# Border changes in a one-core diffusion layer kernel: the order of loads in the first stage, work moved across stage borders, and the end of the output projection

## Chip, cores and metric

The kernel runs on one core of a Trainium2 chip. The metric is the device time in microseconds (us) of one execution. PE is TensorE, DVE is VectorE, ACT is ScalarE, POOL is GpSimd, SP is SyncE, which issues most of the DMAs.

## The reference

One layer of a hybrid diffusion model, in float32: 1024 latent tokens `x` and 256 context tokens `ctx`, 1024 channels wide. Cut to what matters here:

```python
sh1, sc1, g1, sh2, sc2, g2 = modulation(c, w_mod)      # silu(c) @ w_mod + b_mod, in six parts
u_l = modulate(x, norm_g[0], sh1, sc1) @ w_in          # rmsnorm(x) * g * (1 + sc1) + sh1
u_c = modulate(ctx, norm_g[0], sh1c, sc1c) @ w_in      # the same for the context, with c_ctx
# four mixers over column groups of u: GLA, Hyena, Mamba-2, gated DeltaNet
# the end of DeltaNet: head_rmsnorm(o, dn_norm) * silu(og)
# Hyena: x2 * long_conv(x1 * long_conv(v, h0), h1), v, x1, x2 from a conv of three taps,
#        filters h from a three-layer sine network, times a decay window
y = concatenate([gla, hyena, mamba, deltanet]) @ w_out
x = x + g1 * rmsnorm(y, norm_g[1])
h = rmsnorm(x, norm_g[2]) * (1 + sc2) + sh2
x = x + g2 * rmsnorm(ec_moe(h), norm_g[3])             # 16 experts, each takes its best tokens
```

The mixture `ec_moe` takes the softmax over the 16 columns of `h @ moe_router` as affinities, and each expert picks the tokens with the largest.

## The kernel before, in words

The program (L3281) is a row of stages. Each `Stage` is a block of five instruction streams, one for each engine, which are synchronised by semaphores alone and joined by a barrier at its end. Within a stage each engine works through its list in the order written; there is no planner, so what stands before an instruction on its engine is what is written before it. The stages, in order: `mod` (function `modulate`, L197), GLA's two (`gla`, L764), Mamba's, DeltaNet's (`deltanet`, L1423, its scan is the stage `dn_s`, L1779), Hyena's (`hyena`, L2378: `hy_c`, `hy_f`, `hy_d`), `out` (`project_out`, L2734), `moe` (`experts`, L2970) and `fin` (`finish`, L3229).

**mod.** SP issues (L217 to L237), all in one order: for each of eight pieces of `w_mod` (1 MB each) first the token tiles that go with it (tiles 0 to 5 with pieces 0 to 5, tiles 6 and 7 with piece 6, 8 and 9 with piece 7; 0.5 MB each), then the piece; then the mixer weights of GLA (800 columns, 3.2 MB) and two narrow column blocks of 8 and 16 columns, 1024 rows each. The ring of token tiles has four buffers, so tile t waits at L224 until DVE has normalised tile t - 4. ACT squares each tile (L277), DVE scales it (L316), PE turns it with eight transposes (L362), ACT and DVE copy the two halves out (L285, L322). PE multiplies each piece with `silu(c)` (L375). Behind all of them come the row copies (L299 on ACT, L334 on DVE), the 16 transposes that make columns of the modulation rows (L388), and DVE's reduces and adds (L343 to L349).

**gla's first stage.** PE (L849) waits for all mixer weights at once; ACT (L896) and DVE (L944) first scale and shift `hT` by the modulation.

**dn_s.** Ten steps of 128 tokens, both directions in each, are PE products, with ACT and DVE copying between them (ACT: L2020, L2026, L2033; DVE: L2090 writes the output). POOL takes differences of `h` in the earlier steps. **hy_c** is a `project_conv` (L443): six blocks of 128 columns, each product in three passes over a high and a low part of `w` and `hT` (L547 to L549); ACT makes the high part of the first block in four quarters (L527), DVE the low part (L534). Beside it runs `HeadNorm` for DeltaNet's output: ACT's Silu of the gate (L692), POOL's product of gate and weights (L734), DVE's square (L719), reduce, division (L724) and gate product (L729), and 16 transposes (L742) on PE behind the products of block 0. `FilterLayers` (L2306) computes the sine network on the side. Each block's convolution is ACT's centre tap (L633) and two DVE operations (L668, L672), and ACT copies it to `yT` (L595).

**hy_f.** PE makes the filter taps (L2470, L2476), DVE windows them (L2506) and adds the skip at L2514, and PE, ACT and DVE do the transform (L2453, L2563).

**out.** For each of eight tiles of 128 tokens: PE 48 matmuls of 128x512 (L2830 to L2832), ACT the square and root (L2884, L2886), DVE the scaling (L2925), POOL the addition of x, which gives `x1` (L2795), ACT square and root of that (L2889, L2891), DVE the scaling to `h` (L2936), POOL the shift row (L2798). PE turns `h` (L2806) after the next product, multiplies it with the router (L2818) in the middle of the one after, and DVE and ACT take the softmax (L2910 to L2913) whose transpose (L2826) DVE stores (L2945). SP stores `h`. For the last tile DVE does POOL's two additions (L2930, L2940).

**moe and fin.** SP feeds the expert weights through a ring. `fin` loads the sums and the gate row (L3239), and takes the last norm and the residual, tile by tile (L3261 to L3278).

## Time and profile before

| | |
|---|---|
| median of 3 runs | 1836.09 us (1835.57 to 1836.58) |
| the profiled execution | 1830.56 us, its span 1828.7 us |
| mean granted clock of PE | 0.931 |
| DMA over the span | 340.19 MB, 186 GB/s |
| first work of gla's first stage | 54.01 us |
| of hy_f | 888.64 us |
| of moe | 1167.61 us |
| first row load of fin | 1797.63 us |

A time stands in us from the start of the span. "Busy" is the union of an engine's instructions. An idle time stands in front of the instruction that ended it, together with what released it.

### The profile page before, as it was taken

Reading aid. Unit: us, or ns where it says so; the run is one execution under the profiler, and the core shown is the slowest. Engines: PE = TensorE matmul, PEld = TensorE weight load, DVE = VectorE, ACT = ScalarE, POOL = GpSimd, SP = SyncE. Lnnn points to the kernel's source line nnn. Section 1 sums busy time; section 2 is a strip of 40 time slices with the busy share of each in tenths; the row PEclk is TensorE's granted clock in tenths of the full one; section 3 lists DMA queues with packets and bytes.
Section 4 is the critical chain, followed back from the end, with each engine's and each line's share of the span. In section 5 each row is a group of like instructions: output and inputs, shape, how many; then the busy total and the mean of one; then the engine's idle time right before and its main releaser. Section 6 shows DMA issues by size and latency. Waiting matters only on the chain. (4 is left out here: it accounts for less than half of the span.)

```text
span 1828.7 us, 20488 instructions
## 1 busy us (share of the span) xinstructions
PE 1581.6 (86%) x7747; PEld 1179.7 (65%) x7747; DVE 1169.1 (64%) x1338; ACT 887.4 (49%) x1219; POOL 345.1 (19%) x404
## 2 busy tenths in 40 slices
PE   5899999988998869989877799239999999999981
PEld 2454665466556658868457578238888888888860
DVE  3640562249354655765679623678888888888863
ACT  4230334334426546643110245327777777777752
POOL 0000320055002768710000144001001001001001
PEclk9889999988998979999999899569999999999986
DMA  9740200041003753330321422339999999999957
GB/s 365 241 164 1 93 1 0 0 145 41 0 1 106 235 162 91 102 104 0 115 92 39 159 104 81 161 138 375 395 399 384 393 399 394 385 400 395 380 194 206
DMA packets 103000, 340.19 MB, mean 186 GB/s; under 512 B 36295, under 2 KB 41034, under 8 KB 78327
## 3 DMA queue, kind: packets, MB, share of 16 engines
q1 hardware_dynamic: 93022, 315.09, 45.4%
q0 software_dynamic: 5328, 18.88, 4.2%
q10 hardware_dynamic: 4553, 4.92, 1.0%
q8 instruction: 62, 1.02, 0.2%
q14 instruction: 35, 0.29, 0.0%
HBM read 301.52 MB, written 37.32 MB: 185 GB/s over the span
## 5 line engine op out<-in xcount | busy, mean ns | idle before, releaser
L3165 DVE TENSOR_TENSOR w_lo<-w_raw,w_hi 128x2048 fp32r<-128x2048 f32 x192 | 438.4, 2292 | 65.4 <-ACT w_hi L3107 65.4
L3107 ACT ACTIVATE w_hi<-w_raw 128x2048 fp32r<-128x2048 f32 x192 | 368.1, 1918 | 144.6 <-PE ps L3057 134.1
L566 PE MATMUL ps<-hT,w_mixer 128*128 128x512 f32 (+1 forms) x576 | 225.2, 551 | 3.4 <-PEq L177 1.7
L3055 PE MATMUL ps<-w_hi,xsT_hi 128*128 128x512 f32 x512 | 202.8, 396 | 2.4 <-DVE xsT_lo L3170 2.4
L3057 PE MATMUL ps<-w_hi,xsT_lo 128*128 128x512 f32 x512 | 200.4, 391 | 0.0
L3056 PE MATMUL ps<-w_lo,xsT_hi 128*128 128x512 f32 x512 | 200.2, 391 | 0.0
L566 PEld LDWEIGHTS ps<-hT,w_mixer 128*128 128x128 f32 x576 | 109.5, 192 | 110.1 <-issue 106.8
L3023 POOL DMA_INDIRECT moe_sum<-y,idx_col x15 | 30.6, 2040 | 460.7 <-ACT y L3127 460.7
L3055 PEld LDWEIGHTS ps<-w_hi,xsT_hi 128*128 128x128 f32 x512 | 96.8, 189 | 22.0 <-DVE xsT_lo L3170 2.8
L3057 PEld LDWEIGHTS ps<-w_hi,xsT_lo 128*128 128x128 f32 x512 | 96.5, 189 | 20.4
L3056 PEld LDWEIGHTS ps<-w_lo,xsT_hi 128*128 128x128 f32 x512 | 96.7, 189 | 19.3
L3055 PE MATMUL ps<-w_hi,hiddenT_hi 128*128 128x512 f32 x256 | 100.5, 392 | 2.4 <-DVE hiddenT_lo L3182 2.4
L3056 PE MATMUL ps<-w_lo,hiddenT_hi 128*128 128x512 f32 x256 | 100.3, 392 | 0.0
L3057 PE MATMUL ps<-w_hi,hiddenT_lo 128*128 128x512 f32 x256 | 100.2, 392 | 0.0
L888 PE MATMUL ps<-w_mixer,hT 128*128 128x512 f32 (+1 forms) x160 | 64.1, 564 | 0.6 <-ACT mb_dt L925 0.6
L2789 POOL TENSOR_TENSOR yT_lo<-yT,yT_hi 128x1024 fp32r<-128x1024 f32 x7 | 18.5, 2637 | 227.7 <-ACT yT_hi L2869 227.7
L2830 PE MATMUL ps<-w_out_hi,yT_hi 128*128 128x512 f32 x128 | 52.7, 412 | 7.9 <-DVE w_out_lo L2904 5.2
L623 ACT ACTIVATE mb_c_line<-ps 128x512 f32<-128x512 f32 (+1 forms) x20 | 18.2, 909 | 84.5 <-PE ps L566 84.5
L3055 PEld LDWEIGHTS ps<-w_hi,hiddenT_hi 128*128 128x128 f32 x256 | 48.6, 190 | 12.9 <-DVE hiddenT_lo L3182 2.8
L3056 PEld LDWEIGHTS ps<-w_lo,hiddenT_hi 128*128 128x128 f32 x256 | 48.5, 189 | 10.1
L3057 PEld LDWEIGHTS ps<-w_hi,hiddenT_lo 128*128 128x128 f32 x256 | 48.5, 189 | 10.1
L849 PE MATMUL ps<-hT,w_mixer 128*128 128x512 f32 (+1 forms) x128 | 50.1, 554 | 4.7 <-DVE hT L944 4.7
(517 smaller groups left out, 3095.8 us busy)
## 6 DMA issues: line engine op xcount, KB each, us to landing
w_raw<-in_moe_w_gate SPq DMA_DIRECT2D x64, 1024.0 KB, 7.1
w_raw<-in_moe_w_up SPq DMA_DIRECT2D x64, 1024.0 KB, 8.9
w_raw<-in_moe_w_down SPq DMA_DIRECT2D x64, 1024.0 KB, 9.3
w_mod_row<-in_w_mod SPq DMA_DIRECT2D x32, 512.0 KB, 5.2
w_mod<-in_w_mod SPq DMA_DIRECT2D x8, 1024.0 KB, 13.9
w_mixer<-in_w_in SPq DMA_DIRECT2D x4, 2048.0 KB, 11.6
dn_ma<-dn_ma SPq DMA_DIRECT2D x16, 512.0 KB, 3.4
dn_mT<-dn_ma SPq DMA_DIRECT2D x20, 256.0 KB, 3.5
```

Of the source, the lines that this page charges most:

```text
L566: last = nc.tensor.matmul(S.ps[:, 3 * (i % 2) + c, 0:n], S.w[:, k, b["col"]:b["col"] + P], S.hT[:, k, t0:t0 + n], start=(k == 0), stop=(k ...
L623: nc.scalar.activation(d, src, ACT.Copy).then_inc(s.evac, 1)
L849: last = nc.tensor.matmul(S.ps[0:m, q % 6, 0:n], S.w[:, k, col:col + m], S.hT[:, k, t0:t0 + n], start=(x == 0), stop=(x == KD - 1))
L888: last = nc.tensor.matmul(S.ps[:, 5 + i % 3, 0:n], S.hT[:, k, t * P:(t + 1) * P], S.w[:, k, col:col + n], start=(k == 0), stop=(k == KD - 1))
L2789: nc.gpsimd.tensor_tensor(tile_cols(yl, t + 1), tile_cols(S.yT, t + 1), yh[(t + 1) % 2][:, :, :], ALU.subtract).then_inc(s.yl, 1)
L2830: nc.tensor.matmul(out, yh[t % 2][:, k, :], wh[:, k, c], start=(k == 0), stop=False)
L3023: pool.indirect_dma_start(A["moe_sum"], bass.IndirectOffsetOnAxis(ap=S.icol[:, u:u + 1], axis=0), y[:, :], None, compute_op=ALU.add).then_ ...
L3055: nc.tensor.matmul(out, h[:, kk, :], wh[w][:, c:c + 512], start=kk == 0, stop=False)
L3056: nc.tensor.matmul(out, h[:, kk, :], wl[w][:, c:c + 512], start=False, stop=False)
L3057: last = nc.tensor.matmul(out, l[:, kk, :], wh[w][:, c:c + 512], start=False, stop=kk == KD - 1)
L3107: nc.scalar.activation(wh[q % RING][:, :], S.raw[q % RAW][:, :], ACT.Copy).then_inc(s.hi, 1)
L3165: nc.vector.tensor_tensor(wl[q % RING][:, :], S.raw[q % RAW][:, :], wh[q % RING][:, :].bitcast(F32), ALU.subtract).then_inc(s.lo, 1)
```

## The change

In the first stage the token tiles go ahead of the modulation weights by the table `X_WITH`, the two narrow column blocks follow piece 1, and the mixer weights come behind pieces 6 and 7 in column parts; GLA's PE waits for the first 256 columns only and, before the products of the last columns, for the rest. The first modulation row is copied and turned apart from the second. In DeltaNet, ACT takes the Silu of one gate tile per step from the third step on, and POOL multiplies the weights in behind the eighth, both in `dn_s`. In hy_c the square comes before the fourth quarter of the low part. The last block's convolution moves from hy_c into hy_f, and the first filter taps from hy_f to the end of hy_c's PE stream (their sum and difference of weights to its DVE stream). In the out stage PE turns `x1` instead of `h`; the scale row is multiplied into the router (`rs`), the shift row's product with the router becomes a constant (`cb`), and DVE makes the logits from both; the last tile goes in halves, and a root of a constant is taken ahead of the last square. The row loads of `fin` are issued by moe's SP stream, and the last tile of `fin` goes in halves. Cut to its core, each part moved to the left margin:

```diff
 XB, PIECE_K = 4, 2
+X_WITH = ((0, 1), (2, 3), (4, 5), (6,), (7,), (8,), (9,), ())
...
+    for t in X_WITH[i]:
         load_x(t)
     j, k = i // 4, PIECE_K * (i % 4)
     src = A["w_mod"][0, :, j * D:(j + 1) * D].rearrange("(p k) n -> p k n", p=P)
     sp.dma_start(wm[i][:, :, :], src[:, k:k + PIECE_K, :]).then_inc(s.w_in[i], 16)
-load_weights(sp, S, A, 0, GLA_COLS)
-for at, col, n in ((GLA_COLS + 32, MB0 + MB_COLS - 8, 8), (GLA_COLS + 64, DN0 + DN_COLS - 16, 16)):
-    src = A["w_in"][0, :, col:col + n].rearrange("(p k) n -> p k n", p=P)
-    sp.dma_start(S.w[:, :, at:at + n], src).then_inc(S.w_ready, 16)
-    S.w_count += 16
+    if i == 1:
+        load_cols(GLA_COLS + 32, MB0 + MB_COLS - 8, 8, S.w_ready)
+        load_cols(GLA_COLS + 64, DN0 + DN_COLS - 16, 16, S.w_ready)
+sp.wait_ge(s.w_in[6], 16)
+load_cols(0, 0, 256, S.w_first)
+sp.wait_ge(s.w_in[7], 16)
+load_cols(768, 768, GLA_COLS - 768, S.w_ready)
+for h in range(2):
+    load_cols(256 + 256 * h, 256 + 256 * h, 256, S.w_ready)
+S.w_count += 80
...
+if t == 8:
+    act.wait_ge(s.prod, 4)
+    nc.scalar.activation(row[:, 0, :], S.ps[:, 2:4, :].rearrange("p a b -> p (a b)"), ACT.Copy).then_inc(s.row_a, 1)
...
-nc.scalar.activation(row[:, 0, :], S.ps[:, 2:4, :].rearrange("p a b -> p (a b)"), ACT.Copy).then_inc(s.row_a, 1)
+nc.scalar.activation(row[:, 1, 0:512], S.ps[:, 4, :], ACT.Copy).then_inc(s.row_b, 1)
...
-dve.wait_ge(s.prod, 8)
-nc.vector.tensor_copy(row[:, 1, :], S.ps[:, 4:6, :].rearrange("p a b -> p (a b)")).then_inc(s.row_v, 1)
+def cols(j):
+    dve.wait_ge(s.cols_done, j + 1)
+    m = S.ps[:, 2 + 2 * j:4 + 2 * j, :].rearrange("p a (k g c) -> p (a k) c g", k=4, g=4)
+    ch(nc.vector.tensor_reduce(modc[:, j, :, :], m[:, :, 0:2, :], AX.X, ALU.add))
+    for st in range(2):
+        ch(nc.vector.tensor_tensor(modc[:, j, :, st], modc[:, j, :, st], bmod[:, j, :], ALU.add))
 dve.wait_ge(s.pcols_t, 1)
 ch(nc.vector.tensor_copy(S.pcols[:, 0:66], S.ps[:, 7, 0:66]))
 ch(nc.vector.memset(S.pcols[:, 66:69], 0.0))
 ch(nc.vector.memset(S.pcols[:, 67:68], 1.0))
-dve.wait_ge(s.cols_done, 1)
-for j in range(2):
-    m = S.ps[:, 2 + 2 * j:4 + 2 * j, :].rearrange("p a (k g c) -> p (a k) c g", k=4, g=4)
-    for st in range(2):
-        ch(nc.vector.tensor_reduce(modc[:, j, :, st], m[:, :, st, :], AX.X, ALU.add))
+cols(0)
 for st in range(2):
-    ch(nc.vector.tensor_tensor(modc[:, :, :, st], modc[:, :, :, st], bmod[:, :, :], ALU.add))
+    ch(nc.vector.tensor_copy(S.mod1[:, 1, st, :], modc[:, 0, :, st]))
+dve.wait_ge(s.prod, 8)
+nc.vector.tensor_copy(row[:, 1, 512:1024], S.ps[:, 5, :]).then_inc(s.row_v, 1)
+cols(1)
 for st in range(2):
...
+for t in X_WITH[i]:
     turn(t)
...
-pe.wait_ge(s.row_v, 1)
 for j in range(2):
+    if j == 0:
+        pe.wait_ge(s.row_a, 1)
+    else:
+        pe.wait_ge(s.row_b, 1)
+        pe.wait_ge(s.row_v, 1)
     for k in range(KD):
         last = nc.tensor.transpose(S.ps[:, 2 + 2 * j + k // 4, (k % 4) * P:(k % 4 + 1) * P], row[:, j, k::KD],
                                    S.t("ident"))
...
-def split_low(dve, i):
+def split_low(dve, i, quarters=range(4)):
     for x, j in enumerate(QUARTERS if i == 0 else (None,)):
+        if x not in quarters:
+            continue
...
                 col = blocks[i]["col"]
@@ -573,6 +594,10 @@
                 side.pe(s, pe, i)
             if blocks[NB - 1]["tok"] is not None:
                 to_tokens(pe, NB - 1)
+            if later:
+                pe.wait_ge(s.evac, base[NB - 1])
+                pe.wait_ge(s.tok_e, turned[toks[-1]] + len(groups[toks[-1]]))
+                side.end_pe(s, pe)
...
-norm.dve(s, dve, ch)
+    split_low(dve, 0, range(3))
+    norm.dve(s, dve, ch, lambda: split_low(dve, 0, range(3, 4)))
+else:
+    norm.dve(s, dve, ch)
...
 def act(self, s, act):
     nc, st = self.nc, self.st
-    nc.scalar.activation(self.gate[:, :, :], self.gate[:, :, :], ACT.Silu).then_inc(s.sil, 1)
+    if not self.ready:
+        nc.scalar.activation(self.gate[:, :, :], self.gate[:, :, :], ACT.Silu).then_inc(s.sil, 1)
...
+if between is not None:
+    between()
 nc.vector.tensor_reduce(st[:, 0, :], sq[:, :, :].rearrange("p t (h v) -> p (t h) v", v=HV), AX.X, ALU.add
...
-        dve.wait_ge(s.weighed, 1)
+        if not self.ready:
+            dve.wait_ge(s.weighed, 1)
         nc.vector.tensor_tensor(o[:, :, :], o[:, :, :], gate[:, :, :], ALU.mult).then_inc(s.nsq, 1)
 def pool(self, s, pool):
-    if not self.gate_first:
+    if not self.gate_first and not self.ready:
         pool.wait_ge(s.sil, 1)
...
-pe.wait_ge(S.w_ready, S.w_count)
+pe.wait_ge(S.w_first, 16)
 for i, (col, m, dst, _) in enumerate(cms):
+    if dst is lr:
...
+pool.wait_ge(s.gated, LT)
+nc.gpsimd.tensor_tensor(og[:, :, :], og[:, :, :], S.dn_norm[:, :].unsqueeze(1).to_broadcast([P, LT, DG]), ALU.mult)
...
+if 2 <= st < 2 + LT:
+    g = og[:, st - 2, :]
+    nc.scalar.activation(g, g, ACT.Silu).then_inc(s.gated, 1)
...
+def end_pe(self, s, pe):
+    pe.wait_ge(s.sin, 3)
+    pe.wait_ge(s.folded, 2)
+    for q in range(2):
+        self.nc.tensor.matmul(self.ps[0:1, q, 0:DG], self.h[self.rows(q), 0:1], self.w4[self.rows(q), 0:DG],
+                              start=True, stop=True)
+    self.taps(0).then_inc(s.ready, 1)
+    pe.wait_ge(s.ready, 1)
...
+w4 = self.w4
+for d, op in enumerate((ALU.add, ALU.subtract)):
+    nc.vector.tensor_tensor(self.both[:, d, :], w4[:, 0:DG], w4[:, DG:2 * DG], op).then_inc(s.folded, 1)
...
+last = blocks[-1]
+dve.wait_ge(s.centre, 1)
+for j, done in enumerate((s.conv_1, s.conv_2)):
+    at = last["tap"] + 2 * j * last["step"]
+    nc.vector.scalar_tensor_tensor(conv[:, LAT_AT:1283], line[:, LAT_AT - 1 + 2 * j:1282 + 2 * j],
+                                   S.pcols[:, at:at + 1], conv[:, LAT_AT:1283], ALU.mult, ALU.add).then_inc(done, 1)
+    dve.wait_ge(done, 1)
...
+last = blocks[-1]
+at = last["tap"] + last["step"]
+nc.scalar.activation(conv[:, LAT_AT:1283], line[:, LAT_AT:1283], ACT.Identity,
+                     bias=S.pcols[:, last["bias"]:last["bias"] + 1], scale=S.pcols[:, at:at + 1]).then_inc(s.centre, 1)
 act.wait_ge(s.turn_in, 16)
+act.wait_ge(s.conv_2, 1)
+nc.scalar.activation(last["cm"], conv[:, LAT_AT:LAT_AT + SEQ], ACT.Copy).then_inc(s.x2, 1)
...
+for j in range(2):
+    sp.dma_start(rr[KD * j:KD * j + KD, :], A["rows"][1 + j, :].rearrange("(k p) -> k p", p=P)).then_inc(s.rr_in, 16)
...
 def turn_rows(pe, t):
-    pe.wait_ge(s.h2d, t + 1)
     if t >= 1:
         pe.wait_ge(s.ht_a, t)
         pe.wait_ge(s.ht_v, t)
     for k in range(KD):
+        if k == 0 and t == LT - 1:
+            pe.wait_ge(s.x1h, 1)
+        elif k == 0 or k == KD // 2 and t == LT - 1:
+            pe.wait_ge(s.x1d, t + 1)
         last = nc.tensor.transpose(S.ps[:, 4 + k // 4, (k % 4) * P:(k % 4 + 1) * P],
-                                   h2[t % 2][:, k * P:(k + 1) * P], S.t("ident"))
-    last.then_inc(s.tr, 1)
+                                   x1[:, t, k * P:(k + 1) * P], S.t("ident"))
...
 def router(pe, t):
-    pe.wait_ge(s.ht_a, t + 1)
-    pe.wait_ge(s.ht_v, t + 1)
     if t >= 1:
-        pe.wait_ge(s.ex, t)
-    else:
-        pe.wait_ge(s.r_in, 16)
+        pe.wait_ge(s.lgd, t)
     for k in range(KD):
-        last = nc.tensor.matmul(S.ps[:, 6, 0:NE], hT[:, k, :], rt[:, k, :], start=(k == 0), stop=(k == KD - 1))
+        if k % 4 == 0:
+            pe.wait_ge((s.ht_a, s.ht_v)[k // 4], t + 1)
+        last = nc.tensor.matmul(S.ps[:, 6, 0:NE], hT[:, k, :], rs[:, 0, k, :], start=(k == 0), stop=(k == KD - 1))
     last.then_inc(s.lg, 1)
...
 last.then_inc(s.y, 1)
+pe.wait_ge(s.rs, 2)
+for k in range(KD):
+    last = nc.tensor.matmul(S.ps[:, 6, 0:NE], S.ones[:, :], rs[:, 1, k, :], start=(k == 0), stop=(k == KD - 1))
+last.then_inc(s.shift, 1)
+pe.wait_ge(s.shifted, 1)
...
+if t == LT:
+    square_x(act, LT - 1)
+    act.wait_ge(s.tr, 2 * t - 1)
+    nc.scalar.activation(hT[:, 0:4, :], S.ps[:, 4, :].rearrange("p (k c) -> p k c", c=P), ACT.Copy
+                         ).then_inc(s.ht_a, 1)
 if t >= 2:
     u = t - 2
     act.wait_ge(s.mx, u + 1)
-    nc.scalar.activation(sm[u % 2][:, 0:NE], S.ps[:, 6, 0:NE], ACT.Exp, bias=st[:, u, 6:7],
+    nc.scalar.activation(sm[u % 2][:, 0:NE], lt[u % 2][:, :], ACT.Exp, bias=st[:, u, 6:7],
                          accum_out=st[:, u, 7:8]).then_inc(s.ex, 1)
-if 1 <= t <= LT:
-    act.wait_ge(s.tr, t)
+if t == LT - 1:
+    nc.scalar.activation(st[:, t, 7:8], S.eps[:, 0:1], ACT.Sqrt)
+    square_y(act, t)
+if 1 <= t < LT:
...
+if t < LT - 1:
+    square_y(act, t)
+    square_x(act, t)
...
+dve.wait_ge(s.rr_t, 1)
+nc.vector.tensor_copy(rc[:, :, :].rearrange("p j k -> p (j k)"), S.ps[:, 7, 0:2 * KD]).then_inc(s.rc, 1)
+dve.wait_ge(s.rc, 1)
+dve.wait_ge(s.r_in, 16)
+for j in range(2):
+    nc.vector.tensor_tensor(rs[:, j, :, :], rt[:, :, :], rc[:, j, :].unsqueeze(2).to_broadcast([P, KD, NE]), ALU.mult
+                            ).then_inc(s.rs, 1)
...
+def logits(u):
+    dve.wait_ge(s.lg, u + 1)
+    nc.vector.scalar_tensor_tensor(lt[u % 2][:, :], S.ps[:, 6, 0:NE], st[:, u, 2:3], cb[:, :], ALU.mult, ALU.add
+                                   ).then_inc(s.lgd, 1)
+    dve.wait_ge(s.lgd, u + 1)
+    nc.vector.tensor_reduce(st[:, u, 6:7], lt[u % 2][:, :], AX.X, ALU.max, negate=True).then_inc(s.mx, 1)
...
+def normed(t):
+    dve.wait_ge(s.rt2, t + 1)
+    ch(nc.vector.reciprocal(st[:, t, 2:3], st[:, t, 4:5]))
+    if t >= 2:
+        dve.wait_ge(s.h2s[t % 2], 16 * (t // 2))
+    nc.vector.scalar_tensor_tensor(h2[t % 2][:, :], x1[:, t, :], st[:, t, 2:3], rows[:, 1, :],
+                                   ALU.mult, ALU.mult).then_inc(s.h2m, 1)
...
+        if t == 0:
+            dve.wait_ge(s.shift, 1)
+            nc.vector.tensor_copy(cb[:, :], S.ps[:, 6, 0:NE]).then_inc(s.shifted, 1)
+        normed(t)
+        if t >= 3:
+            store(t - 3)
+        continue
+    dve.wait_ge(s.x_in[t % 2], 16 * (t // 2 + 1))
+    for h in range(2):
+        c = slice(h * 512, h * 512 + 512)
+        nc.vector.scalar_tensor_tensor(tm[t % 2][:, c], S.ps[:, 2 * (t % 2) + h, :], st[:, t, 2:3], rows[:, 0, c],
+                                       ALU.mult, ALU.mult).then_inc(s.y_sc, 1)
+        dve.wait_ge(s.y_sc, LT + h)
+        nc.vector.tensor_tensor(x1[:, t, c], tm[t % 2][:, c], xt[t % 2][:, c], ALU.add
+                                ).then_inc((s.x1h, s.x1d)[h], 1)
+store(LT - 4)
+logits(LT - 2)
+turn(LT - 1)
+dve.wait_ge(s.x1h, 1)
+dve.wait_ge(s.x1d, LT)
+normed(LT - 1)
+store(LT - 3)
+affinity(LT - 2)
+dve.wait_ge(s.h2m, LT)
+nc.vector.tensor_tensor(h2[(LT - 1) % 2][:, :], h2[(LT - 1) % 2][:, :], rows[:, 2, :], ALU.add).then_inc(s.h2l, 1)
+logits(LT - 1)
+affinity(LT - 1)
+store(LT - 2)
+store(LT - 1)
...
+sp.wait_ge(S.y_added, NE * 16 + 16)
+for t in range(LT):
+    sp.dma_start(S.m[t][:, :], A["moe_sum"][t * P:(t + 1) * P, :]).then_inc(S.m_in[t], 16)
+    if t == 0:
+        sp.dma_start(S.g[:, :], A["rows"][3, :].partition_broadcast(P)).then_inc(S.g_in, 16)
...
+for h in range(2):
+    sp.wait_ge(s.out, LT - ADDED + h)
+    c = slice(h * 512, h * 512 + 512)
+    sp.dma_start(A["out"][0, (LT - 1) * P:, c], m[LT - 1][:, c]).then_inc(s.st, 16)
...
+if t == LT - 1:
+    for h in range(2):
+        c = slice(h * 512, h * 512 + 512)
+        nc.vector.scalar_tensor_tensor(m[t][:, c], m[t][:, c], st[:, t, 2:3], g[:, c], ALU.mult, ALU.mult
+                                       ).then_inc(s.sc, 1)
+        dve.wait_ge(s.sc, LT + h)
+        nc.vector.tensor_tensor(m[t][:, c], m[t][:, c], S.x1[:, t, c], ALU.add).then_inc(s.out, 1)
```

## Rows read from the trace of the kernel before

**Rows 1.** the page: busy time of each engine, its share of the span, instructions
```profile
PE 1581.6 (86%) x7747; PEld 1179.7 (65%) x7747; DVE 1169.1 (64%) x1338; ACT 887.4 (49%) x1219; POOL 345.1 (19%) x404
```

**Rows 2.** windows: us, PE, PEld, DVE, ACT, POOL busy (x), PEclk, DMA share, GB/s
```profile
35.00:40.00 5.00, 3.21 (x20) 1.75 (x21) 1.92 (x5) 1.58 (x5) 0.00 (x0) 1.00 1.04 399
47.50:49.50 2.00, 1.26 (x10) 1.29 (x11) 0.85 (x4) 0.28 (x1) 0.00 (x0) 0.91 1.12 239
```

**Rows 3.** timeline 0 to 56, first stage: start us, us, engine line op [idle before <-releaser]
```profile
10.94 1.92 PE L375 MATMUL ps<-w_mod,silu_padded 128*32 128x512 f32 x4 [10.94 <-DMA w_mod<-in_w_mod]
...
42.34 1.91 PE L375 MATMUL ps<-w_mod,silu_padded 128*32 128x512 f32 x8 [1.65 <-DMA w_mod<-in_w_mod]
46.88 1.22 DVE L334 COPY mod_rows<-ps 128x1024 f32<-128x1024 f32 x1
48.24 2.95 PE L388 MATMUL ps<-tables,mod_rows 128*128 128x128 f32 x16 [0.88 <-DVE mod_rows L334]
54.01 2.37 ACT L896 ACTIVATE hT<-hT,mod 128x1024 f32<-128x1024 f32 x2 [6.23 <-PEq L185]
```

**Rows 4.** timeline of hy_c's head, 801 to 818
```profile
801.53 0.43 DVE L534 TENSOR_TENSOR w_mixer_lo<-w_mixer,w_mixer_lo 128x256 fp32r<-128x256 f32 x1 [4.04 <-ACT w_mixer_lo L527]
...
804.81 4.62 POOL L734 TENSOR_TENSOR dn_og<-dn_og,dn_norm 128x2048 f32<-128x2048 f32 x1 [8.62 <-ACT dn_og L692]
807.26 4.33 DVE L724 TENSOR_TENSOR dn_o<-dn_o,dn_n_stat 128x2048 f32<-128x2048 f32 x1
811.62 2.29 DVE L729 TENSOR_TENSOR dn_o<-dn_o,dn_og 128x2048 f32<-128x2048 f32 x1
813.97 3.49 PE L742 MATMUL ps<-tables,dn_o 128*128 128x128 f32 x16 [4.38 <-DVE dn_o L729]
```

**Rows 5.** timeline between hy_c and hy_f, 887 to 895
```profile
887.33 1.06 ACT L595 ACTIVATE yT<-hy_c_conv 128x1024 f32<-128x1024 f32 x1 [2.67 <-DVE hy_c_conv L672]
888.69 1.01 PE L2470 MATMUL ps<-hy_fw,hy_h 64*1 64x256 f32 x4 [5.95 <-PEq L185]
894.08 0.68 DVE L2514 TENSOR_TENSOR hy_taps<-ps,hy_window 1x512 f32<-1x512 f32 x1 [1.02 <-DMA hy_skip<-in_hy_d]
```

**Rows 6.** timeline of the out stage, 1047 to 1166
```profile
1047.51 1.28 DVE L2925 SCALAR_TENSOR_TENSOR res_tmp<-ps,out_stats,row_broadcasts 128x1024 f32<-128x1024 f32 x1
...
1056.87 1.09 PE L2806 MATMUL ps<-tables,h 128*128 128x128 f32 x8 [1.53 <-POOL h L2798]
1059.17 0.55 PE L2830 MATMUL ps<-w_out_hi,yT_hi 128*128 128x512 f32 x1 [1.22 <-POOL yT_lo L2789]
...
1145.94 1.03 PE L2806 MATMUL ps<-tables,h 128*128 128x128 f32 x8
1148.63 1.28 ACT L2886 ACT_TABLE_LOAD   x1
1165.88 0.28 DVE L2945 COPY affT<-ps 32x128 f32<-32x128 f32 x1 [0.79 <-PE ps L2826]
```

**Rows 7.** window in fin (columns as in rows 2)
```profile
1804.00:1808.00 4.00, 0.00 (x0) 0.00 (x0) 3.23 (x6) 3.38 (x7) 1.09 (x2) 0.50 1.03 422
```

**Rows 8.** timeline of dn_s: one step's first ACT copy, DVE's last result
```profile
708.92 0.66 ACT L2033 ACTIVATE dn_wT<-ps 128x256 f32<-128x256 f32 x2 [1.46 <-PE ps L1912]
...
794.16 0.42 DVE L2090 TENSOR_TENSOR dn_o<-dn_oq,ps 128x256 f32<-128x256 f32 x1
```

**Rows 9.** source line L724, at its call for mb: min/median/max ns, start
```profile
L724 DVE TENSOR_TENSOR mb_o<-mb_o,mb_n_stat x1: 2292/2292/2292, 457.1 to 457.1; 128x2048 f32<-128x2048 f32 x1
```

**Rows 10.** windows in hy_c and out (columns as in rows 2)
```profile
814.00:819.30 5.30, 5.30 (x20) 3.89 (x20) 1.09 (x2) 3.60 (x6) 0.00 (x0) 0.70 0.06 16
1044.50:1056.90 12.40, 10.87 (x49) 8.67 (x47) 2.90 (x4) 5.08 (x8) 4.84 (x3) 1.00 0.26 103
1059.20:1066.00 6.80, 6.80 (x23) 5.44 (x24) 1.96 (x4) 2.72 (x7) 2.38 (x1) 0.75 0.41 139
```

**Rows 11.** SP's waits, 0 to 150: us in total, times, longest us
```profile
SPq L224 <- DVE x_norm L316: 20.5, 6, 4.6
```

217 lines of the change are left out of this document (113 added, 104 removed).

## The prediction

> **What bounds the kernel now.** I read the page first: PE is busy 86% of the span [rows 1], far ahead of the others, so the time goes where PE stands idle or works at a low granted clock. Such places are short and lie at the borders of the stages, each closed by a barrier, so that what is won at one border adds to what is won at the next. Then I read the timeline around each border that the diff touches, and asked there which wait ends last. In the first stage it is the DMA: share 1.04 at 399 GB/s [rows 2], and PE waits 1.65 us for the last piece of w_mod, which it takes up at 42.34 [rows 3]. After it come 11.7 us of turning, copying and reducing until the next stage's ACT starts at 54.01 [rows 3]. At the head of hy_c PE stands 4.38 us for the gated norm on DVE [rows 4]; between hy_c and hy_f it stands 5.95 us for a convolution's tail [rows 5]; and the out stage ends with a serial chain from 1145.94 to 1166.16 [rows 6]. The fin stage is bound by DMA (share 1.03, 422 GB/s) [rows 7].
>
> All sums are made against the profiled execution (1830.56 us, span 1828.7). The median of the runs is 5.53 us above it; I take the same shift for the changed kernel.
>
> **First stage: gain 1.4.** Before, two tiles are turned behind the last product (42.34 + 1.91 = 44.25); both row halves are copied whole (1.22) when that is done, 16 transposes take 48.24 to 51.19, and DVE's ten short operations and the barrier take the 2.8 to 54.01 [rows 3]; I give the barrier 0.65 of it. Now no tile is turned behind the last product, the first row is copied long before, and the rest goes in two rounds: but DVE takes them in order. I estimate, from these rows: products end 44.25; turn of the parameters 0.25 and eight transposes (half of 2.95) to 46.0; DVE's reduce, two adds and two copies, half of the 2.1, to 47.1; only then its half-row copy (half of 1.22) to 47.8; eight transposes to 49.3; reduce, adds and the final products 1.1 to 50.4; barrier 0.65 to 51.1. That is 2.9 earlier than 54.01. Against it, two loads of 1024 packets of 32 and 64 bytes move from the end of the queue to a place before the last six pieces. Where they pass now, the DMA engines move 239 GB/s at share 1.12 [rows 2], and the time lost against 399 is 0.8 us in that window, with their last part behind it: I take 1.5, bounds 0.5 and 2.5. So 2.9 - 1.5 = 1.4, bounds 0.4 and 3. The mixer weights now start behind pieces six and seven. Their first 256 columns (1 MB, 2.6 us at 399 GB/s) follow the last piece and land near 48, before PE wants them at about 53; the products of the last columns wait for the rest, about 3.2 MB or 8 us behind 44, and come later still. SP issues these loads before its barrier; the queue has taken the last of them when about half is through, near 48.5, ahead of 50.4.
>
> **dn_s and the head of hy_c: gain 5.5.** Each of dn_s's steps gets a Silu of 128x256 on ACT (0.33, as its copies of that shape) in front of work that ends with 1.46 us idle before L2033 [rows 8]: hidden, and one table load (1.28, as L2886 [rows 6]) with the first. The gate-weight product (4.62 on POOL [rows 4]) moves behind the last Silu, about 786 to 791, before DVE's last result at 794.58 [rows 8]: hidden, if POOL is free as the trace has it, else up to 2 of it shows. In hy_c, DVE now squares (2.29, as L729 of the same shape) before it waits for ACT's fourth quarter and not behind it. DVE stood 4.04 us in that wait, so the square is hidden in it; L534 still runs 801.53 to 801.96, and L724, which started at 807.26, starts 2.29 earlier, at about 805.0. L724 took 4.33 there and 2.29 for the same shape with POOL idle [rows 4, 9]: with POOL's product gone it ends at 807.3, L729 (2.29) at 809.65. PE's products end at 813.97 - 4.38 = 809.59, so 4.2 of the 4.38 go. The 16 transposes took 3.49, and the clock stood at 0.70 (between its levels 1.2 and 2.4 GHz) in 814 to 819.3 [rows 4, 10], 1.6 us lost in those 5.3; without the pause I take back 1.3. Sum 5.5, bounds 3.5 and 6.
>
> L724's 4.33 ended 2.16 after POOL's end at 809.43: the rows show the DVE operation standing until POOL was through. The Trainium skill ("SBUF — State Buffer", section "SBUF: two separate sides") says of the port pair that DVE and GpSimd share that one side holds the port for the whole instruction and the other blocks. By that rule POOL's 4.62 could hold up a DVE operation with two SBUF inputs in dn_s in its place, and the gain would be smaller by up to what one of them waits; the rows of dn_s that end last read PSUM on one side [rows 8], so I leave the sum.
>
> **hy_c's tail into hy_f: gain 2.5.** PE ended at 888.69 - 5.95 = 882.74 and the barrier came after ACT's copy at 888.39 [rows 5]. The conv of the last block (ACT centre, two DVE operations) and that copy move into hy_f; in their place stand an evacuation of 0.6 and four matmuls of end_pe, with it about 2.3, so hy_f starts at 885.3 instead of 888.64 (table above). Its DVE chain is set by hy_skip's load (894.08, 5.4 after the start), which moves along: 3.3. PE's clock is low after the idle time and more of the work now lies there: 0.9 lost, an estimate from the 1.3 of the same kind above. Net 2.5, bounds 1.5 and 3.5. The moved conv (2.6 on DVE) and copy (1.06) fall into DVE's idle time before the even sums; if that cover were gone, up to 1.
>
> **Out stage: gain 4.7.** At its start PE gets eight matmuls of ones with the scaled router and then waits for `shifted`. DVE gives that behind its first scaled product, which ran 1047.51 to 1048.79 [rows 6], so about 1049.1. Queued behind the wait on PE is all of product 1, which could start at about 1044.5: 4.6 lost, and 1.75 more in low clock, as in 1059.2 to 1066 (0.75 over 6.8 us [rows 10]). Given back are that same slow stretch (1.7) and PE's two waits in front of it (1.53 for POOL's h and 1.22 for yT_lo [rows 6]), since x1 is turned now and not h, and PE is late anyway. 4.6 + 1.75 - 1.7 - 1.53 - 1.22 = 1.9 lost. The end: from the last product (1145.94) to affT's copy (1166.16) 20.2 us [rows 6], and 1.45 to the start of moe (1167.61 in the table above). Now the root's table is loaded ahead (1.28 [rows 6]), x1 comes in halves (2.7 for four operations in place of 1.28 + 1.23, but the first is ready 3.4 behind the last product's end: square and root 1.6, DVE's turn copy and reciprocal 0.4, half of both operations 1.35), it is turned at once, and the router (at half clock some 3.5) runs beside the second square, its root and h. Counted on from the product's end: x1 4.75, its root 6.35, hT copied 6.95, router to 10.5, softmax 11.95, turned and stored 13.0; h2's add ends 10.35 and its store near 13.2; with 1.45, 14.7 against 21.7. Gain 6.9; less 1.9 and 0.3 for the new short operations, 4.7. Bounds 1 (the starting stall whole, a router's path that waits for DVE) and 7.
>
> **Fin: gain 0.3.** The row loads are issued by the stage before, 0.25 earlier, and the last tile leaves in halves. DMA is full there [rows 7], which hides the halves' extra operation. Bounds 0 and 0.8.
>
> Sum 1.4 + 5.5 + 2.5 + 4.7 + 0.3 = 14.4: 1816.2 profiled, 1821.7 as a median.
>
> **The rivals.** *Clocks and waits eat more* (0.16): router and hy_f at low clock, POOL's product in DVE's way, the small loads dear: the lower bounds give 0.4 + 3.5 + 1.5 + 1 + 0 = 6.4, time 1829.7. For it: wherever PE stands now, a stretch at 0.70 to 0.75 follows [rows 10]. *All bounds on the good side* (0.12): half way to the upper bounds 17.4, 1818.7; all the way 20.3, 1815.8. *The x ring runs late* (0.05): SP waits for DVE before six tiles, 20.5 us in sum, longest 4.6 [rows 11], harmless while the queue is full. With tiles ahead of pieces fewer bytes stand behind each wait. By the pace of the queue (13 MiB in all, 11.5 of them between 10.94 and 42.34, 2.73 us each [rows 3]) six tiles and three pieces, 6 MiB, would land at 10.94 + 4.5 x 2.73 + 1.5 for the narrow loads = 24.7, so the queue is empty some 2 earlier, near 22.9, if the seventh tile isn't issued by then; I reckon it at 20.2, since it waits for the fourth tile's scaling, two turns behind product 0. Each us after 22.9 costs one: with 3 to 6, 1826. *The Silus cost a table switch each* (0.03), if something between them wants another table: 8 x (2 x 1.28 + 0.33 - 1.46) = 11.4, time 1833.1.
>
> *Slower* (0.04): the new stall on PE, 4.6 us at 1044.5, leaves the clock at 1.2 GHz through the products behind it. One product is 10.87 us of PE at clock 1.00 [rows 10]; two at half clock add 21.8 and not the 1.75 of my sum, so 14.4 - 20 = -5.6, time 1841.7. It decides from (14.4 + 1.75) / 10.87 = 1.5 products at half clock. Against it: after the 4.38 us wait at 813.97 the clock was back within the 5.3 us shown (0.70 as their mean) [rows 10].
>
> That the change doesn't do what it says would show as products of hy_c waiting as before; parts are independent, so this only lowers the gain (in the first rival).
>
> **How the numbers follow.** Forecast 0.60, with its own range 1818 to 1825. 1821.7 is its time, and the range runs from the upper bounds' time to that of the lower ones, 1815 to 1830. A measurement of this kernel can tell about 0.2%, 3.7 us, from no change: slower than that holds the clock's case, 0.04; within it the switches' case and part of the first rival, 0.04; faster the rest, 0.92.
>
> **What would show it.** Right: gla's first ACT operation near 52.6; PE's wait before L742's transposes under 0.5 and L724 at 2.3; hy_f's start 2.6 behind hy_c's last product instead of 5.9; one PE wait of about 2.8 to 4.6 after product 0, none for yT_lo at product 2; 14 to 15 us from the last product to moe's first issue. Wrong: DMA share under 1 before the last w_mod piece; a table load at each Silu; clock 0.5 through product 1; and a total gain under 6 or over 21.

## The result and the profile after

The changed kernel takes 1813.56 us as the median of 4 runs (1810.01 to 1815.68), the kernel before 1835.83; the ratio is 0.9886 (95% interval 0.9871 to 0.9901). By the ratio it is 21 us faster (18 to 24), by the two medians 22.3. The prediction was 1821.7 with a range of 1815 to 1830: right in sign, too small in size, and the measured time lies 1.4 us below the range. The profiled execution took 1813.14 us (span 1811.3), that of before 1830.56 (1828.7).

The page of the changed kernel, engines' busy time (PE was at 1581.6 us [rows 1]):

```profile
PE 1580.1 (87%) x7764; PEld 1181.3 (65%) x7764; DVE 1169.3 (65%) x1354; ACT 887.1 (49%) x1228; POOL 343.9 (19%) x404
```

PE does the same work; what went is time in which it stood. So the reading that helps is the one by stage. The next table takes the time from the first instruction of a stage to that of the next one, from six profiled executions of the kernel before (the one above and five more, e1 and e14 to e17) and two of the changed kernel (the one above and e13):

| stage | before, mean (lowest, highest) | after, two profiles | gain | forecast |
|---|---|---|---|---|
| first stage | 54.7 (52.2, 58.4) | 55.1, 55.7 | -0.6 | +1.4 |
| gla's to dn_a | 599.9 (598.2, 601.1) | 601.6, 600.0 | -0.8 | 0 |
| dn_s | 141.4 (140.8, 142.1) | 142.1, 141.6 | -0.5 | 8.0, with the next two rows |
| hy_c | 92.9 (90.9, 96.2) | 82.8, 82.8 | +10.1 | |
| hy_f and hy_d | 139.0 (138.3, 140.0) | 139.6, 139.6 | -0.6 | |
| out | 139.9 (139.3, 140.2) | 133.1, 133.1 | +6.8 | 4.7 |
| moe, to its last scatter | 622.1 (621.9, 622.3) | 621.4, 621.4 | +0.8 | 0 |
| from there to the end | 38.9 (38.8, 39.1) | 35.8, 35.8 | +3.1 | 0.3 |
| sum | 1828.8 | 1810.6 | 18.2 | 14.4 |

The gains are taken from unrounded times. Among the six profiles of the kernel before, moe and the end repeat within 0.4 us, out within 1.0, dn_s, hy_f and hy_d within 1.7. The first stage, the stretch to dn_a and hy_c vary by 3 to 6 us between executions of one kernel, so differences of 1 us there say nothing by themselves.

**First stage.** Timeline of the changed kernel, 44 to 56 (it answers to [rows 3]; there the last product started at 42.34):

```profile
46.90 1.91 PE L391 MATMUL ps<-w_mod,silu_padded 128*32 128x512 f32 x8
48.86 1.11 PE L407 MATMUL ps<-tables,mod_rows 128*128 128x128 f32 x8
51.45 0.69 DVE L361 COPY mod_rows<-ps 128x512 f32<-128x512 f32 x1 [0.33 <-DVE mod L359]
52.28 1.13 PE L407 MATMUL ps<-tables,mod_rows 128*128 128x128 f32 x8 [2.32 <-DVE mod_rows L361]
55.09 1.24 ACT L932 ACTIVATE hT<-hT,mod 128x1024 f32<-128x1024 f32 x1 [5.63 <-PEq L185]
```

The last product comes 4.6 later than before. Behind it the work is shorter, 8.2 us instead of 11.7, and as the prediction said the row copy on DVE (51.45) waits for the parameter copy and the first column group, PE's second eight transposes for it. The windows of the same stretch (columns as in [rows 2]):

```profile
15.00:20.00 5.00, 5.00 (x26) 3.09 (x24) 1.08 (x3) 1.93 (x4) 0.00 (x0) 1.00 1.19 239
25.00:30.00 5.00, 3.90 (x24) 2.23 (x24) 3.03 (x6) 3.06 (x8) 0.00 (x0) 1.00 0.92 330
40.00:45.00 5.00, 4.03 (x22) 1.73 (x24) 1.52 (x3) 2.04 (x4) 0.00 (x0) 1.00 0.85 340
```

From 15 to 20 the engines of the DMA are busier than full (share 1.19) and move 239 GB/s instead of the 400 around it: there the two narrow loads pass. From 25 to 30 the queue is thin (330 GB/s). From 40 to 45 it drains (340): SP waits there for the last pieces before it issues the mixer weights. SP's own row shows a second cost of the narrow loads, beside their time in the queue:

```profile
5.96 7.97 SPq L229 DMA_DIRECT2D w_mixer<-in_w_in  x2
```

Their issue holds SP until 13.9, so that the next token tile goes out at 13.97 (at 11.08 in e3 below, which issues them last). And the last product no longer waits for its piece: that lands at 46.44, while PE still turns the last tile (1.16 us), so the product starts 0.46 behind the landing. In the kernel before it was 0.04.

**Head of hy_c** (answers to [rows 4]): DVE's and PE's rows.

```profile
800.18 2.29 DVE L750 TENSOR_TENSOR dn_n_sq<-dn_o 128x2048 f32<-128x2048 f32 x1
804.13 2.28 DVE L753 TENSOR_REDUCE dn_n_stat<-dn_n_sq 128x32 f32<-128x2048 f32 x1
807.19 2.29 DVE L757 TENSOR_TENSOR dn_o<-dn_o,dn_n_stat 128x2048 f32<-128x2048 f32 x1
809.52 2.29 DVE L763 TENSOR_TENSOR dn_o<-dn_o,dn_og 128x2048 f32<-128x2048 f32 x1
812.12 1.91 PE L776 MATMUL ps<-tables,dn_o 128*128 128x128 f32 x16
```

No wait stands in front of the transposes L776: PE reaches them 13.4 us into the stage, 4.6 earlier than before, they take 1.91 instead of 3.49, and the clock has not fallen (columns as in [rows 2]):

```profile
812.00:817.00 5.00, 5.00 (x27) 3.33 (x26) 1.93 (x2) 4.62 (x7) 0.00 (x0) 1.00 0.35 103
```

L757 takes 2.29, where L724 took 4.33.

**hy_f** (answers to [rows 5]):

```profile
886.92 0.68 DVE L2577 TENSOR_TENSOR hy_taps<-ps,hy_window 1x512 f32<-1x512 f32 x1 [4.21 <-DMA hy_skip<-in_hy_d]
889.50 6.29 PE L2403 MATMUL ps<-hy_fw_both,hy_h 64*128 64x512 f32 x16 [5.61 <-DVE hy_taps L2569]
```

DVE stands 4.21 us for the small load hy_skip, behind it PE stands 5.61, and the sixteen matmuls that follow take 6.29, with the clock near its lower level:

```profile
889.50:895.80 6.30, 6.29 (x16) 2.00 (x16) 4.35 (x4) 0.00 (x0) 0.00 (x0) 0.58 1.07 383
```

**out** (answers to [rows 6]): PE's wait for the shift column, the last product's end, the last store; then the window behind that wait.

```profile
1041.87 0.79 PE L2915 MATMUL ps<-w_out_hi,yT_hi 128*128 128x512 f32 x1 [2.79 <-DVE router_shift L3067]
...
1139.35 1.03 PE L2892 MATMUL ps<-tables,x 128*128 128x128 f32 x8
...
1152.27 0.28 DVE L3041 COPY affT<-ps 32x128 f32<-32x128 f32 x1 [0.79 <-PE ps L2911]
```

```profile
1041.90:1048.00 6.10, 6.10 (x21) 4.95 (x22) 1.45 (x2) 2.40 (x4) 2.93 (x2) 0.75 0.01 3
```

From the last product's end to moe's first instruction (1154.10) are 14.75 us, forecast 14.7. The stall at the start is there too, 2.79, and product 1 starts 20.9 us into the stage instead of 17.0. Yet the last product ends 118.35 us into the stage, and 118.48 before: all of it is made up.

**The end.** The last scatter of moe, the first row load and fin's first ACT operation, of the kernel before, and then of the changed one:

```profile
1789.81 1.55 POOL L3029 DMA_INDIRECT moe_sum<-y,idx_col  x1 [3.36 <-ACT y L3160]
1797.63 0.33 SPq L3239 DMA_DIRECT2D moe_rows<-moe_sum  x1
1801.13 1.06 ACT L3261 ACTIVATE moe_sq<-moe_rows 128x1024 f32<-128x1024 f32 x1 [11.59 <-DMA moe_rows<-moe_sum]
```

```profile
1775.48 1.55 POOL L3188 DMA_INDIRECT moe_sum<-y,idx_col  x1 [3.36 <-ACT y L3319]
1780.32 0.33 SPq L3163 DMA_DIRECT2D moe_rows<-moe_sum  x1
1785.18 1.06 ACT L3418 ACTIVATE moe_sq<-moe_rows 128x1024 f32<-128x1024 f32 x1 [9.97 <-PEq L185]
```

From scatter to load 7.82 became 4.84, and to ACT's start 11.32 became 9.70.

### The profile page after: what moved, and what is told of

Its sections match the earlier page's. It is cut to its first block and busy times, and to the rows that moved or that the text cites. A ratio compares the mean times of both kernels' runs of the same rounds, so it can differ in the third digit from the quotient of the medians.

```text
span 1811.3 us, 20557 instructions
## 1 busy us (share of the span) xinstructions
PE 1580.1 (87%) x7764; PEld 1181.3 (65%) x7764; DVE 1169.3 (65%) x1354; ACT 887.1 (49%) x1228; POOL 343.9 (19%) x404
## 3 DMA queue, kind: packets, MB, share of 16 engines
q8 instruction: 62, 1.02, 0.2%
## 5 line engine op out<-in xcount | busy, mean ns | idle before, releaser
L3216 PEld LDWEIGHTS ps<-w_hi,xsT_lo 128*128 128x128 f32 x512 | 96.4, 188 | 20.2
L648 ACT ACTIVATE mb_c_line<-ps 128x512 f32<-128x512 f32 (+1 forms) x20 | 18.2, 909 | 84.5 <-PE ps L587 84.5
L3216 PEld LDWEIGHTS ps<-w_hi,hiddenT_lo 128*128 128x128 f32 x256 | 48.5, 189 | 10.1
```

Of the source, the lines that this page charges most:

```text
L648: nc.scalar.activation(d, src, ACT.Copy).then_inc(s.evac, 1)
L3216: last = nc.tensor.matmul(out, l[:, kk, :], wh[w][:, c:c + 512], start=False, stop=kk == KD - 1)
```

## The experiments

All are against the kernel before on the same chip; medians are theirs, and stage times come from their profiles. One run has a spread of some 3 us, so for parts of 1 to 4 us the stage times decide. Each edit is to the changed kernel, unless it says otherwise.

**e1, e13 to e17: the two kernels again.** No edit.

> The kernel before, unchanged, for a second profile. The profiled execution of before was 1830.56 us where its runs had a median of 1835.83. If that execution was a quick one, this profile shows a span near 1833 to 1836, and the stage in which it is longer says where executions differ (my guess: moe, the longest DMA-fed stage). Rival: the profile is again near 1830 and the medians are 5 us above what a profiled execution takes.

> The changed kernel itself. If the missing 4 to 5 us are spread between executions, its profile again shows 54 to 58 for the first stage, and the stages behind it within 0.5 of the first profile but for the one before dn_s (266 to 271), and the medians of one call differ by 17 to 21. Rival: a cost that profiles don't show; the medians then differ by 20 to 21 again, the profiles by 14 to 16.

> The kernel before itself, a third profile. Spread: its profile lies anywhere between 1827 and 1841, and with three profiles the mean comes nearer to the median of the executions. Rival: the profile is near 1829 again, 5 under the median of the other executions.

> The kernel before, a fourth profile. If the long stretch at the lower clock behind the wait in hy_c is common, at least two of e15 to e17 show hy_c at 95 to 97 us; if it was a rare event, all show 92 to 93.

> The kernel before, a fifth profile; hy_c at 95 to 97 us if the long stretch at the lower clock is common, 92 to 93 if it was rare.

> The kernel before, a sixth profile; hy_c at 95 to 97 us if the long stretch at the lower clock is common, 92 to 93 if it was rare.

Measured: before 1833.31 (e1) and 1834.35 (e14), ratio to further runs of the same kernel 0.9995 (0.9982 to 1.0008) and 1.0008 (0.9993 to 1.0022); spans of the five profiles 1825.2, 1828.7, 1829.7, 1827.8 and 1833.0. The changed kernel (e13) 1811.84, ratio 0.9887 (0.9866 to 0.9908), its profile 1810.0. The six profiles of before have a mean span of 1828.8, 18.2 above the two of the changed kernel, which is the sum of the stages. The other 2 to 3 us of the 21 are not placed by any stage. One candidate showed up in e14, hy_c at 96.2 where four others have 92.4 to 92.7 and e16 has 90.9: windows of e14, of the first profile of before and of e16 at about the same place, each some us behind PE's wait for the gated norm:

```profile
816.00:822.00 6.00, 6.00 (x12) 3.26 (x11) 4.97 (x6) 1.80 (x2) 0.00 (x0) 0.50 0.57 178
```

```profile
818.00:824.00 6.00, 6.00 (x25) 4.17 (x23) 4.64 (x5) 2.17 (x3) 0.00 (x0) 1.00 0.55 178
```

```profile
816.00:822.00 6.00, 6.00 (x23) 3.97 (x22) 4.10 (x4) 2.74 (x4) 0.00 (x0) 1.00 0.53 178
```

Same kernel, same work, and the clock is at 0.50, its lower level, in e14 and at 1.00 in the two others. The six profiles differ in how long the low stretch behind this wait lasted: none in e16, some 3 us in four of them, some 10 us in e14. Their hy_c follows it: 90.9, then 92.4 to 92.7, then 96.2. What decides on the length stays open. e15 to e17 didn't repeat e14's (92.4, 90.9, 92.7): one in six, 3.7 us, is under 1 us on average. My guess of e1, that the spread sits in moe, was wrong: moe is the steadiest stage.

**e2: the first stage as before,** with gla's one wait.

```diff
-pe.wait_ge(S.w_first, 16)
+pe.wait_ge(S.w_ready, S.w_count)
...
-for t in X_WITH[i]:
+for t in (i,) if i < 6 else (2 * i - 6, 2 * i - 5):
```

> The changed kernel with the first stage and gla's single wait as before. Theory: the new first stage costs (its end came at 55.06 instead of 54.01, and gla's first stage loses another 0.7 to a low clock), so this is 1.5 to 2.5 us faster than the changed kernel, gla_s starting near 189.3. Rival, my forecast: the new first stage gains 1.4, so this is 1.4 slower than the changed kernel.

Measured: 1815.41, ratio 0.9894 (0.9877 to 0.9911). The last product starts at 41.77 and the stage ends at 53.8, where nine profiles with the new stage have 54.8 to 57.8, mean 55.7. With the six of before the old order has a mean of 54.6, 1.1 less, with a standard error of 0.8: the forecast gain of 1.4 didn't come, and whether the new stage costs 1 us or nothing can't be told, by the medians neither. The loss in gla that I expected to go is spread (134.9 to 136.4 with the new order, 135.0 to 136.2 with the old).

**e3: the narrow loads behind the mixer weights.**

```diff
-if i == 1:
-    load_cols(GLA_COLS + 32, MB0 + MB_COLS - 8, 8, S.w_ready)
-    load_cols(GLA_COLS + 64, DN0 + DN_COLS - 16, 16, S.w_ready)
...
     load_cols(256 + 256 * h, 256 + 256 * h, 256, S.w_ready)
+load_cols(GLA_COLS + 32, MB0 + MB_COLS - 8, 8, S.w_ready)
+load_cols(GLA_COLS + 64, DN0 + DN_COLS - 16, 16, S.w_ready)
```

> The changed kernel with the two narrow column loads back behind the mixer weights. Theory: their 2048 small packets hold the DMA queue for about 3 us ahead of the last pieces of w_mod, so the last product starts 2.5 to 4 us earlier than 46.90 and the time falls by 2.5 to 4. Rival (the x ring: tiles issued too late leave the queue empty): the last product moves by under 1 us, and windows with a DMA share under 0.95 stay between 25 and 45.

Measured: 1813.77, ratio 0.9895 (0.988 to 0.991); the stage ends at 52.8, 2.9 ahead of the mean of the nine. Window and last product:

```profile
15.00:20.00 5.00, 4.70 (x33) 3.05 (x32) 2.21 (x4) 3.04 (x6) 0.00 (x0) 1.00 1.03 403
```

```profile
43.80 1.91 PE L390 MATMUL ps<-w_mod,silu_padded 128*32 128x512 f32 x8
```

The stretch at 239 GB/s is gone and the last product, 43.80, comes 3.1 earlier than in the first profile (46.90) and than the mean of the ten profiles with the same loads, which spread from 45.09 (e4) to 48.92. The window 25 to 30 still has 328 GB/s, and the product is still 2.0 behind e2's. Of these 2.0, the last piece lands 1.7 later (43.36 against 41.70) and PE's turn of the last tile in front of the product takes the rest. So both theories hold: the narrow loads with about 3 us at the product and by the stage's end, tiles that are issued late with up to 1.7. The figures of e2 and e3 are from one profile each.

**e4: the row copy first on DVE.**

```diff
+dve.wait_ge(s.prod, 8)
+nc.vector.tensor_copy(row[:, 1, 512:1024], S.ps[:, 5, :]).then_inc(s.row_v, 1)
 dve.wait_ge(s.pcols_t, 1)
...
-dve.wait_ge(s.prod, 8)
-nc.vector.tensor_copy(row[:, 1, 512:1024], S.ps[:, 5, :]).then_inc(s.row_v, 1)
 cols(1)
```

> The changed kernel with DVE's copy of the second row's half ahead of the parameter copy and the first column group. Theory: the second eight transposes wait for DVE's order (row copy at 51.45, 2.6 us behind the last product), so they start 2 us earlier, the stage ends 1.3 to 2 us earlier, and PE's clock in gla's first stage drops less, up to 0.5 more. Rival: the stage's end is set by SP, which issues the mixer weights until about 50 to 54, and nothing is gained.

Measured: 1811.55, ratio 0.9883 (0.9868 to 0.9898). PE's last product and its transposes:

```profile
45.09 1.91 PE L391 MATMUL ps<-w_mod,silu_padded 128*32 128x512 f32 x8 [0.37 <-DMA w_mod<-in_w_mod]
47.04 2.01 PE L407 MATMUL ps<-tables,mod_rows 128*128 128x128 f32 x16
```

Now the sixteen transposes run in one go behind the product, and from its start to the end of the stage (50.95) are 5.9 us instead of 8.2. The order on DVE cost the change 2.3. That its product starts at 45.09 is the spread: nothing in the edit comes before it.

**e5: the out stage as before** (whole function).

```diff
-                                   x1[:, t, k * P:(k + 1) * P], S.t("ident"))
-            if k % 4 == 3:
-                last.then_inc(s.tr, 1)
+                                   h2[t % 2][:, k * P:(k + 1) * P], S.t("ident"))
+        last.then_inc(s.tr, 1)
...
-                last = nc.tensor.matmul(S.ps[:, 6, 0:NE], hT[:, k, :], rs[:, 0, k, :], start=(k == 0), stop=(k == KD - 1))
+                last = nc.tensor.matmul(S.ps[:, 6, 0:NE], hT[:, k, :], rt[:, k, :], start=(k == 0), stop=(k == KD - 1))
...
-            pe.wait_ge(s.shifted, 1)
```

> The changed kernel with the whole out stage as before. Theory: the stage took 133.1 us in the changed kernel and 140.15 before; the stall at its start is made up because PE no longer waits for POOL later on, and the end gives 6.9. So the stage takes 139.5 to 140.5 again and the kernel is 7 slower than the changed one. Rival, my forecast: 4.7 slower, with 2 of it lost at the start.

Measured: 1818.15, ratio 0.9928 (0.99 to 0.9956); the stage took 139.4 instead of 133.1, 6.3 more. The theory had 139.5 to 140.5; the medians differ by 4.6, with a spread that takes 6.3 in.

**e6: the shift column waited for late.**

```diff
-pe.wait_ge(s.shifted, 1)
 for t in range(1, LT + 3):
...
     pe.wait_ge(s.lgd, t)
+else:
+    pe.wait_ge(s.shifted, 1)
```

> The changed kernel, but PE waits for the router's shift column only ahead of the first router product, so product 1 starts at once behind product 0 and the eight small products. Theory: the 2.8 us wait goes and product 1 runs at full clock, but PE then waits for POOL's yT_lo in later tiles as in the kernel before, so that of the 4.3 won at the start 1 to 3 us stay; the stage takes 130.5 to 132. Rival A: PE is the bound all through, all 4.3 stay (128.8). Rival B: POOL's chain sets the pace and nothing stays (133).

Measured: 1809.41, ratio 0.9881 (0.9849 to 0.9913). The stage takes 130.3: 2.8 of it go, a bit more than the theory's middle; PE then waits 2.1 us for POOL's yT_lo, which was 0.8. But moe takes 623.5 instead of 621.4. Its first products, ten us from 50 us into the stage, in e6 and in the changed kernel:

```profile
1199.10:1209.10 10.00, 8.40 (x25) 6.69 (x26) 8.68 (x5) 2.21 (x2) 0.43 (x1) 0.62 0.69 248
```

```profile
1204.10:1214.10 10.00, 8.40 (x31) 6.84 (x32) 9.68 (x5) 3.35 (x3) 0.43 (x1) 0.77 0.71 241
```

The clock is 0.62 instead of 0.77. By DVE's rows the stage is 1.3 of its 2.1 us behind at 84 us, and the rest comes bit by bit later. In e12 and e18 below the same ten us have 0.63 and 0.77. That the lower clock is the cause is read from this and not tested; why it is lower stays open.

**e7: fin's row loads in fin; e8: five of eight.** The edit of e7 (the gate row moves too):

```diff
-sp.wait_ge(S.y_added, NE * 16 + 16)
-for t in range(LT):
-    sp.dma_start(S.m[t][:, :], A["moe_sum"][t * P:(t + 1) * P, :]).then_inc(S.m_in[t], 16)
...
+for t in range(0, LT):
+    sp.dma_start(m[t][:, :], A["moe_sum"][t * P:(t + 1) * P, :]).then_inc(S.m_in[t], 16)
```

and of e8:

```diff
-for t in range(LT):
+for t in range(3):
     sp.dma_start(S.m[t][:, :], A["moe_sum"][t * P:(t + 1) * P, :]).then_inc(S.m_in[t], 16)
...
+for t in range(3, LT):
+    sp.dma_start(m[t][:, :], A["moe_sum"][t * P:(t + 1) * P, :]).then_inc(S.m_in[t], 16)
```

> The changed kernel with fin's row loads issued by fin again; its last tile stays in halves. Theory: from the last scatter's issue to the first row load it was 7.8 us before and is 4.8 now, because POOL's stream comes out of its last wait and through the barrier about 3 us later than SP's semaphore wait; so the first load comes 7.8 behind the scatter again, ACT starts 1.5 to 1.8 later and the kernel is 2 to 3 us slower. Rival, my forecast: 0.25 to 0.3 slower.

> The changed kernel with three row loads and the gate row issued by moe's SP stream and five by fin's. Theory: fin's start is now held by SP's issue of nine loads (4.4 us of 9.7 behind the scatter); with four issues the barrier is set by POOL's stream at 7.8 behind the scatter, ACT starts 1.5 to 1.9 earlier, but the DMA queue is full soon after and the end moves by 0 to 1. Rival: the end moves with the start, 1.5 to 1.9 earlier.

Measured: e7 1817.56, ratio 0.9918 (0.989 to 0.9946); 7.96 from scatter to load and 39.2 from scatter to end, 3.4 more than with the loads in moe. The trace shows what lies between. In the kernel before the scatter lands 4.6 us behind its issue, and POOL goes past its wait at once; then it executes the DRAIN with which it ends the stage:

```profile
L185 POOLq DRAIN  x1: 2755/2755/2755, 1794.6 to 1794.6; - x1
```

That is from 4.8 to 7.6 behind the scatter's issue; the signals of the barrier behind it take 0.2. e7 has the same DRAIN of 2755 ns in the same place. So has the changed kernel, but there SP is past its own wait at 4.8 and issues the loads beside it. e8 1815.08, ratio 0.991 (0.9881 to 0.9939): ACT starts 8.1 behind the scatter, not 9.7,

```profile
1784.82 1.06 ACT L3420 ACTIVATE moe_sq<-moe_rows 128x1024 f32<-128x1024 f32 x1 [8.40 <-DMA moe_rows<-moe_sum]
```

and the end comes 36.0 behind it, as without: the start alone is worth nothing. In both the last tile goes in halves, and e7, with the halves alone, ends 39.2 behind the scatter as the kernel before does (38.9): the halves gave none of the 3.1.

**e9: the tail of hy_c and the head of hy_f as before** (`FilterLayers` and `hyena`).

```diff
-line, conv = project_conv(..., weights=S.hy_w, later=True)
+project_conv(..., weights=S.hy_w)
```

> The changed kernel with the tail of hy_c and hy_f as before (last convolution in hy_c, first taps and their weights in hy_f). Theory: of the 9.5 us that dn_s to hy_f's start gained, 3.2 are this part, of which hy_f gives back 1.9; the stretch from dn_s's start to hy_f's start takes 228 instead of 224.8, hy_f 52.3 instead of 54.2, and the kernel is 1.2 to 2 us slower. Rival: the part gives its 3.2 whole and hy_f's loss has another cause (it stays 54.2).

Measured: 1817.17, ratio 0.9925 (0.991 to 0.994). hy_c takes 87.2 (82.8), hy_f 52.4 (54.2), hy_d 86.4 (85.4): the part gives 4.4 in hy_c and loses 0.8 behind it, 3.6 in all. PE stands 5.9 us in front of hy_f again. The ten edited kernels that keep this hy_c have 82.9 to 83.8, mean 83.3, so the 4.4 can be 3.9 and the 3.6 can be 3.1. The expectation's 1.2 to 2 was too low.

**e10: the gate back in hy_c.**

```diff
-pool.wait_ge(s.gated, LT)
-nc.gpsimd.tensor_tensor(og[:, :, :], og[:, :, :], S.dn_norm..., ALU.mult)
...
-if 2 <= st < 2 + LT:
-    g = og[:, st - 2, :]
-    nc.scalar.activation(g, g, ACT.Silu).then_inc(s.gated, 1)
...
-(3, 4, 6, 7), ready=True)
+(3, 4, 6, 7))
```

> The changed kernel with the Silu of the gate on ACT and the product with its weights on POOL back in hy_c (its square still ahead of the fourth quarter). Theory: L724's successor takes 4.3 again instead of 2.29 because POOL's 4.6 us product runs beside it, PE waits 2 to 2.5 us behind block 0 and its clock drops; 3 to 4.5 us slower. Rival: the gate was not on the path (with the square earlier, DVE waits for nothing else); under 1 us.

Measured: 1822.55, ratio 0.9946 (0.993 to 0.9961), hy_c 89.0, 6.2 more. POOL, DVE and PE:

```profile
811.05 4.64 POOL L768 TENSOR_TENSOR dn_og<-dn_og,dn_norm 128x2048 f32<-128x2048 f32 x1 [8.76 <-ACT dn_og L723]
813.03 4.82 DVE L757 TENSOR_TENSOR dn_o<-dn_o,dn_n_stat 128x2048 f32<-128x2048 f32 x1
...
820.22 3.37 PE L776 MATMUL ps<-tables,dn_o 128*128 128x128 f32 x16 [4.56 <-DVE dn_o L763]
```

The expectation had 3 to 4.5, too low: PE waits 4.56 in all, and the transposes take 3.37 instead of 1.91 at a low clock. They start 18.2 us into the stage, as before (18.0; 13.4 in the changed kernel). So all of the head's 4.6 is gone with the gate, although the square still runs early: moved alone, it gives nothing. L757 ends at 817.85, 2.16 behind POOL's end at 815.69, to the hundredth what L724 did in the kernel before. In dn_s the same POOL product ran from 788.32 to 792.84 in the changed kernel, and the four operations that DVE began inside it, each with one input in PSUM, took their usual times. The Trainium skill says ("SBUF — State Buffer", section "SBUF: two separate sides") that a GpSimd operation that reads SBUF, as this one does, and a DVE operation with two SBUF inputs exclude each other for the whole instruction. Both readings agree with it. The other case that it names, DVE's 2-port modes, no run here tests.

**e11: the skip term later on DVE.**

```diff
-if n == 0:
+if n == 3:
     dve.wait_ge(s.tapped, 1)
     dve.wait_ge(s.d_in, 16)
...
-pe.wait_ge(s.skipped, 1)
+pe.wait_ge(s.skipped, 2)
```

> The changed kernel, with DVE's skip term in hy_f three tap products later, so that DVE doesn't stand 4.2 us for the small load hy_skip behind its first product. Theory: this wait is what the stage's head hangs on: PE's wait of 5.6 us behind its second tap pair goes, and with it the stretch at clock 0.5; hy_f takes 49 to 51 instead of 54.2. Rival: the transforms wait for the tables hy_dft anyway and nothing moves.

Measured: 1807.65, ratio 0.9873 (0.9858 to 0.9889); hy_f takes 48.6 instead of 54.2.

```profile
882.62 4.85 DVE L2569 TENSOR_TENSOR hy_taps<-ps,hy_window 128x1024 f32<-128x1024 f32 x4 [5.44 <-PEq L185]
888.11 0.68 DVE L2577 TENSOR_TENSOR hy_taps<-ps,hy_window 1x512 f32<-1x512 f32 x1 [0.64 <-DMA hy_skip<-in_hy_d]
```

DVE makes four tap products in a row, its wait is 0.64, the clock in 882.6 to 890 is 1.00. The head of the changed kernel's stage hung on that small load. In the kernel before DVE stood 1.02 us for it; there it was not tried.

**e12: all of it,** that is the edits of e3, e4, e6 and e11 and those below; **e18:** the same without e6, with the shift's wait where the change has it.

```diff
-X_WITH = ((0, 1), (2, 3), (4, 5), (6,), (7,), (8,), (9,), ())
+X_WITH = ((0,), (1,), (2,), (3, 4), (5, 6), (7, 8), (9,), ())
-sp.wait_ge(s.w_in[6], 16)
-sp.wait_ge(s.w_in[7], 16)
```

> The changed kernel with: the narrow loads last; one tile per piece first and none behind the last; no wait ahead of the mixer loads; the row copy first; the shift column waited for late; the skip term later. Theory: the first stage ends near 49 to 50 instead of 55.1, the out stage takes 130.3 instead of 133.1, hy_f 50 instead of 54.2: 10 to 13 us faster than the changed kernel. Rival: moe's loads and the clocks give part of it back, 5 to 8.

> The combined kernel with the shift column's wait where the change put it. Theory: out takes 133.2 instead of 130.2, and if moe's 623.6 (621.4 in all others of the changed kernel) belongs to the late wait, moe takes 621.4 again, so the kernel is only 0.8 slower than the combined one. Rival: moe's 2 us are spread between executions, and it is 3 slower.

Measured: e12 1805.06, ratio 0.985 (0.9835 to 0.9865), span 1799.3; e18 1802.75, ratio 0.9834 (0.9817 to 0.9852), span 1799.1. The first stage ends at 49.8 and 49.4, hy_f takes 48.6 in both. out takes 130.3 in e12 and 133.0 in e18, and moe 623.6 and 621.4: most of the late wait's gain comes back as moe's loss, as in e6. With the new table of tiles the window 25 to 30 has 389 and 392 GB/s instead of e3's 328, and the last piece lands at 42.45 and 41.90 instead of 43.36: 0.9 and 1.5 of what the late tiles cost. Both beat the changed kernel by 11 us in the profiles, about 9 in the medians.

## Why the prediction was wrong

**Two steps failed. The larger one is the shift from profile to median, "I take the same shift for the changed kernel"; the other is the size of four terms of the gain.** The forecast of 1821.7 lies 8.1 us above the measured time. 5.1 of them are the shift: 5.53 was added to the profiled time, and the changed kernel's median lies 0.42 above its own profile. The other 3.0 are the gain, 14.4 forecast, 17.4 between the two profiled executions (18.2 over all eight). Most mechanisms behind the terms were right; the first stage's gain didn't come, and fin's had a path that was not in the sum.

*The shift of 5.53 us* was carried over from one profile and three runs. Over six profiles (mean 1830.7) and 82 runs (mean 1833.5) of the kernel before it is about 3; for the changed kernel it was 0.4 and 0. The three runs lay 2.6 above the mean of all, which is the spread of runs. The 2 to 3 us by which the gain in runs exceeds the gain in profiles stay open. With 0.42 in place of 5.53 the same sum gives 1816.6. The range was built from bounds of terms and didn't have this spread in it.

*Fin, 0.3 forecast, 3.1 measured: of the gains the one furthest off.* The step that failed is "the row loads are issued by the stage before, 0.25 earlier". I took the barrier's own length. What lies in front of the barrier wasn't read: in the kernel before POOL waits for the same semaphore and then joins the barrier, and from the scatter to the first load are 7.8 us; SP's own wait on that semaphore needs 4.8. The difference is POOL's DRAIN of 2.75 us behind its wait, and not its wake-up (e7). The bound of 0.8 was too low for the same reason. An earlier start of the loads moves the whole stretch in which the DMA is full (e7); an earlier start of ACT alone does nothing (e8). The halves of the last tile, the term's second part, gave nothing.

*Out, 4.7 forecast, 6.8 measured.* The end was right (14.7, 14.75), link by link: x1 is there 4.7 us behind the last product's end (forecast 4.75), the router done at 10.4 (10.5), the last store at 13.2 (13.0). "1.9 lost" at the start was wrong: PE's work set the pace, its waits for POOL in later tiles had room for all of the 3.8 us, since PE no longer turns h. PE's waits for yT_lo in the stage, before and after:

```profile
PE ps L2830 <- POOL yT_lo L2789: 2.7, 3, 1.2
PE ps L2915 <- POOL yT_lo L2872: 0.8, 2, 0.6
```

With the 1.53 for h before, 4.2 us became 0.8. I gave back the two waits and the slow stretch that I saw and no more. The "0.3 for the new short operations" didn't show.

*dn_s to hy_d, 8.0 forecast, 9.1 measured.* The tail of hy_c gave 3.1 to 3.6 (e9), not 2.5; its 0.9 lost behind it was right in size (0.8). Its cause was the wait for hy_skip, which the text had named as what sets DVE's chain: 4.21 us on DVE, 5.61 on PE, and a clock of 0.58 behind it. The head of hy_c is the rest, 5.5 to 6.0, forecast 5.5: no wait in front of the transposes, L757 at 2.29, ACT's Silus hidden in dn_s with one table load for all eight. The sum had the square's move give 2.29 by itself; with the gate in hy_c it gives nothing (e10), since POOL's end sets L757's.

*First stage, 1.4 forecast, none measured* (1.1 lost, standard error 0.8). The chain behind the last product was right (DVE's order and all: 8.2 us here, 8.8 there). Before it, the narrow loads cost about 3 (e3), not 1.5 (the bound was 2.5); that they hold SP until 13.9 was not in the sum. The x ring, a rival at 0.05 whose price was put at zero in the sum, cost 0.9 to 1.7 (e2, e3, e12, e18), and the turn of the last tile in front of the last product some 0.4. That rival had each us behind 22.9 cost one, and the seventh tile issued at 20.2, so nothing; it was issued at 20.6, ahead of 22.9, and the rate fell to 330 GB/s in 25 to 30 all the same. The prediction waited for an empty queue; that a thin one moves less was not in it.

*Moe, 0 forecast, 0.8 measured.* 0.5 of it is there at 84 us into the stage: in the ten us from 50 on, the clock is 0.72 in the kernel before and 0.77 in the changed one. Why, and where the rest comes from, is not explained.

Of the rivals, the good side's (0.12) was nearest, though all its bounds give 1815.8; that of the clock staying at 1.2 GHz through two products did not happen: the window behind the new stall shows 0.75.

## What to carry to other kernels

At a stage's border read the last row of the stage before on every queue, POOL's and its DRAIN among them, and not the barrier's own length: take the time from the event that all wait for to the next stage's first instruction. A stall added to the bound engine is free only as far as later waits of the same engine had room for it, and then all of it is; add up these waits before costing the stall. Put loads with rows of 32 or 64 bytes behind everything that the DMA-bound stretch waits for. Before a forecast of 1% is given as a time, take several profiles and runs of the kernel before: the shift between the two was the largest error here.

## What the runs showed of the hardware

- The clock behind a pause is not the same in each execution: behind the same wait of the kernel before (2.7 to 4.4 us) it stayed at 1.00 in one of six profiles, was at 0.50 for some 3 us in four and for some 10 us in one; hy_c took 90.9, 92.4 to 92.7 and 96.2 us (e16; before, e1, e15, e17; e14).
- Two loads of 1024 packets of 32 and 64 bytes, 0.1 MB together, held the DMA at 239 GB/s and share 1.19 for a window of five us and SP in their issue for 8 us; the stage ended 2.9 us later than without them (e3).
- A semaphore wait on SP saw the last scatter land 4.8 us behind its issue (4.6 to 4.9 in thirteen profiles); by the way through POOL's own wait and the barrier the first load was issued 7.8 to 8.0 behind it (seven profiles). 2.75 us of this is POOL's DRAIN, which stands behind POOL's wait for the scatter (before, e7). What it waits for, no run shows.
- A DVE operation with two SBUF inputs, 2.29 us by itself, ended 2.16 us behind the end of the POOL product that ran when it began, in two kernels (before, e10).
- 2.8 us won at the start of the out stage were followed by 2.1 us lost in the next stage, 1.3 of them by 84 us, with a lower clock 50 us into it (e6; 2.2 in e12); e18, without that gain, has moe at 621.4 again.
